# Latent attention's scores: two heads per unit of the order of weights in place of one, its second group one unit later

## The reference, cut to what matters

```python
q_lat = jnp.einsum('bshd,hld->bshl', qh, w_uk)
...
_, idx = lax.top_k(score, k_sel)
...
logits = jnp.einsum('bqhl,bqkl->bqhk', qlb, c_sel).astype(jnp.float32) * (DSA_HEAD_DIM ** -0.5)
...
p = jax.nn.softmax(logits, axis=-1).astype(c.dtype)
o_lat = jnp.einsum('bqhk,bqkl->bqhl', p, c_sel)
o = jnp.einsum('bqhl,hld->bqhd', o_lat, w_uv)
```

## Time and profile before

| what | us |
|---|---|
| median of 3 runs (1111.29 to 1111.47) | 1111.39 |
| span of the profiled execution | 1109.4 |
| TensorE busy in it | 1100.7 (99%) |
| VectorE busy | 744.2 (67%) |
| ScalarE busy | 506.9 (46%) |
| GpSimd busy | 19.8 (2%) |

### The profile page before, as it was taken

The page is one execution under the profiler, slowest core; times in us unless marked ns, Lnnn a source line. Parts: engine busy times, 40 slices in busy tenths (PEclk is TensorE's granted clock), DMA queues, the critical chain, the costliest instruction groups (busy, mean ns, idle before and its releaser), DMA issues.

```text
span 1109.4 us, 18066 instructions
## 1 busy us (share of the span) xinstructions
PE 1100.7 (99%) x7344; PEld 931.1 (84%) x7344; DVE 744.2 (67%) x1195; ACT 506.9 (46%) x851; POOL 19.8 (2%) x40
## 2 busy tenths in 40 slices
PE   9999999999999999999999999999999999999997
PEld 8888888888888888878888887887789999999986
DVE  6875876864686247448789896447568677667853
ACT  7562354324675225533342434336544444444543
POOL 1000000000001001000000000000000000000000
PEclk9999999999999999999999999999999999999999
DMA  9543324432215433522223232231121322333241
GB/s 372 220 149 125 125 68 133 127 102 73 74 58 167 139 95 111 185 74 79 77 76 95 77 95 68 66 114 58 58 73 61 114 93 80 115 115 114 81 186 76
DMA packets 33618, 121.09 MB, mean 109 GB/s; under 512 B 3824, under 2 KB 3824, under 8 KB 33536
## 3 DMA queue, kind: packets, MB, share of 16 engines
q1 hardware_dynamic: 30672, 109.88, 29.7%
q0 software_dynamic: 2720, 10.03, 2.7%
q10 hardware_dynamic: 144, 0.03, 0.0%
HBM read 115.74 MB, written 4.19 MB: 108 GB/s over the span
## 4 chain that ended last, share of the span: by engine, by line
PE 98%; DMA 1%; DVE 1%; ACT 0%; SPq 0%; issue 0%; ACTq 0%
PE acc L1829 22%; PE acc L1831 21%; PE acc L1830 21%; PE acc L1841 2%; PE side L1841 2%; PE acc L1839 2%; PE side L1839 2%; PE acc L1837 2%; PE side L1837 2%; PE acc L2189 2%; PE side L1829 2%; PE side L1830 2%; PE side L1831 2%; PE side L2071 2%; PE side L1984 2%; PE side L2189 1%
## 5 line engine op out<-in xcount | busy, mean ns | idle before, releaser
L1160 DVE TENSOR_TENSOR w_lo<-raw,w_hi 128x1024 fp32r<-128x1024 f32 (+2 forms) x194 | 225.8, 1165 | 149.7 <-ACT w_hi L649 146.8
L1829 PE MATMUL acc<-hT_hi,w_hi 128*128 128x512 f32 x648 | 258.9, 400 | 0.0
L1831 PE MATMUL acc<-hT_hi,w_lo 128*128 128x512 f32 x648 | 252.8, 390 | 0.0
L1830 PE MATMUL acc<-hT_lo,w_hi 128*128 128x512 f32 x648 | 252.4, 390 | 0.0
L649 ACT ACTIVATE w_hi<-raw 128x1024 fp32r<-128x1024 f32 (+2 forms) x194 | 195.6, 1009 | 115.4 <-PE acc L1831 87.7
L1829 PEld LDWEIGHTS acc<-hT_hi,w_hi 128*128 128x128 f32 x648 | 121.9, 188 | 26.9 <-issue 2.9
L1831 PEld LDWEIGHTS acc<-hT_hi,w_lo 128*128 128x128 f32 x648 | 121.6, 188 | 26.1
L1830 PEld LDWEIGHTS acc<-hT_lo,w_hi 128*128 128x128 f32 x648 | 121.9, 188 | 23.6
L1829 PE MATMUL acc<-w_hi,hT_hi 128*128 128x512 f32 (+1 forms) x152 | 60.3, 396 | 0.0
L1831 PE MATMUL acc<-w_hi,hT_lo 128*128 128x512 f32 (+1 forms) x152 | 58.8, 387 | 0.0
L1830 PE MATMUL acc<-w_lo,hT_hi 128*128 128x512 f32 (+1 forms) x152 | 58.7, 386 | 0.0
(11 more groups left out here) (461 smaller groups left out, 2251.5 us busy)
## 6 DMA issues: line engine op xcount, KB each, us to landing
raw<-in_ga SPq DMA_DIRECT2D x32, 512.0 KB, 4.5
ada_raw<-in_ada SPq DMA_DIRECT2D x16, 512.0 KB, 11.5
raw<-in_wo SPq DMA_DIRECT2D x16, 512.0 KB, 3.5
raw<-in_br SPq DMA_DIRECT2D x16, 512.0 KB, 3.5
raw<-in_q SPq DMA_DIRECT2D x8, 512.0 KB, 3.5
raw<-in_u SPq DMA_DIRECT2D x8, 512.0 KB, 4.0
raw<-in_gp SPq DMA_DIRECT2D x8, 512.0 KB, 4.5
raw<-in_ada_w SPq DMA_DIRECT2D x8, 512.0 KB, 3.6
```

The source lines that it names most:

```text
L1160: nc.vector.tensor_tensor(out=lo[:, 0:width], in0=strip_of(k), in1=hi[:, 0:width].bitcast(f32), op=ALU.subtract).then_inc(lo_made, 1)
L1829: nc.tensor.matmul(ps, w[0], x[0], start=first, stop=False)
L1830: nc.tensor.matmul(ps, w[0], x[1], start=False, stop=False)
L1831: return nc.tensor.matmul(ps, w[1], x[0], start=False, stop=last)
```

## The change

```diff
-    SCORES_AT[(1, 9, 19, 27)[_s // 4] + _s % 4 if _s < SPARSE else 38 + (_s - SPARSE) // 2].append(_s)
+    SCORES_AT[(1, 10, 19, 27)[_s // 4] + _s % 4 // 2 if _s < SPARSE else 38 + (_s - SPARSE) // 2].append(_s)
```

## The result

The changed kernel takes 1123.74 us (median of 4 executions, 1123.54 to 1124.94) against 1111.39 before (median of 4 executions, 1111.29 to 1111.47): 12.35 us more, a ratio of 1.0113 with a 95% interval of 1.0102 to 1.0125. Forecast were 1119.8 and a range up to 1123.0. The sign was right, and the time lies above the range.

The account below looks back on a forecast made before the run. PE, busy 99% of the span, was taken as the bound. Stops 0.4 + 3.5 + 2.4 + 0.5 + 2.6 + 0, less gains 0.45 and 0.5, make 8.45 us: 1111.39 + 8.4 = 1119.8, range 1116.0 to 1123.0.

Parts of the forecast that it names:

- The stops: In slots with two turns, PE's second turn waits until ACT has copied the first out of bank side2.
- slot 2: Between turn 0 and turn 1, ACT's round trip of 0.73 us leaves PE a stop of 0.4 us.
- slot 3: Turn 3 waits for ACT's copy, which stands behind DVE's layer norm statistics: stop 3.5 us, between 3.1 and 3.9.
- slot 11: Turn 5 waits for ACT's copy, which stands behind DVE's gate product: stop 2.4 us, between 1.5 and 2.8.
- slot 12: Turn 7 waits for ACT's copy, by the same computation as slot 11: stop 0.5 us.
- slot 20: Turn 9 waits for ACT's copy, made later by slot 19's second score: stop 2.6 us, between 2.0 and 3.0.
- Slot 21: No stop, as ACT has no result to take out and PE three things ahead, 1.65 us.
- The 0.45 at `sel`: In slot 27, PE's wait for the top-k result goes: 0.3 us shown idle and 0.16 more, 0.45 won.
- fewer switches: Eight of sixteen logits no longer have a panel behind them, 0.09 us each: 0.5 us won, between 0 and 0.7.
- The clock falls: Rival: slot 3's 3.5 us stop lowers TensorE's clock; 1122.5 us with half a panel slowed, 1125 whole; chance 0.06.
- catch up: Rival: PE's stops give DVE and ACT time; slot 3's stays, others halve or nearly go: 1116 to 1117.4 us; chance 0.10.
- only the round trip counts: Rival: prompt ACT copies leave stops of 0.2 to 0.5 us; if PE hides these too, 1110.4 us; chance 0.05.

Follow-up runs that it names:

- a wait alone: Kernel before, no score moved, with PE waiting at the end of slot 3's side work until ACT has copied that slot's turn: 1116.47 us.
- two halves: Changed kernel, with the two turns of a slot in blocks 0 and 1 put into the two halves of bank side2: 1115.3 us.
- three-block kernel: Kernel before, with blocks 0, 1 and 3 paired, block 3 from slot 28, and blocks 0 and 1 using both halves of side2: 1111.12 us.
- filled kernel: Changed kernel, with matmuls of no use in the stops, 13 in slot 3 and 9 in slot 20: 1120.69 us.
- kernel with the copies first: Changed kernel, with ACT copying the turns before its wait for DVE's statistics in slot 3 and gate product in slots 11, 12, 20: 1112.98 us.
- block 0 alone: Kernel before, with only block 0's scores two to a slot (slots 1, 1, 2, 2): 1116.94 us.
- half-filled: Changed kernel, with 5 matmuls of no use in slot 3's stop and 9 in slot 20's: 1122.46 us.
- copies of slot 3 first: Changed kernel, with ACT making slot 3's copies of the turns before it waits for DVE's statistics: 1119.45 us.
- block 2 alone: Kernel before, with only block 2's scores two to a slot (slots 19, 19, 20, 20): 1115.2 us.

## Why the prediction was right or wrong

**The stops.** Right, in place, cause and size. Forecast and measured, in us: slot 2, 0.4 and 0.40; slot 3, 3.5 and 3.49; slot 11, 2.4 and 2.36; slot 12, 0.5 and 0.50; slot 20, 2.6 and 2.68; slot 28, 0 and no wait in the list. In slot 3 both ends of the stop came 0.25 us later than forecast, so its length stayed. Slot 21 was given nothing, because ACT has no result to take out and PE three things ahead, and lost 0.26: the forecast left out that the copy waits for the first of PE's two sums there to free the buffer. The cause of the five stops is shown: a wait alone costs the same, two halves of the bank take it away, and so does the order of ACT's queue.

**What is won.** The 0.45 at `sel` was right. The 0.5 for fewer switches was not there. In the changed kernel the logits that follow logits in slot 1 take 0.28 us to their last product (497.90 to 498.18) where the first take 0.22: part of the switch is paid at the next float32 product, be it a panel's or a score's. In the three-block kernel, with six of the eight switches gone, 0.16 us is left, no more than its noise.

**The sum.** Without the clock the changed kernel stands 9.2 us over the one before (filled kernel), where the sum said 8.45. That would have been 1120.6, inside the range. Two ends of terms do not follow from what the prediction says, though nothing rests on them: slot 11's own bounds for the second score (0.4 and 1.5) give a stop of 2.2 to 3.3, not 1.5 to 2.8, and the low ends of all terms add up to 5.85 at the least, not 5.7.

**The clock.** This is the step that failed. "The clock falls" was a rival with 6 in 100 and had to be part of the forecast: it costs 3.05 us at the median and 4.5 in the profiled execution, and the sum had nothing for it. Two things in that step were wrong. From 2 us of idle at 1.00 at the end of the program it took that an idle of 2 us "leaves" the clock; the row only says that the clock had not fallen yet within those 2 us, and the runs show that it falls after PE has resumed, behind an idle shown as 2.16 us. It looked at slot 3 alone, though slot 20's stop was forecast at 2.6. Its price for one fall, half a panel slowed or 2.7 us, was fair, where the slowed stretches cost 1.3 to 2.8 each; the whole panel, 5.5, was too much. The Trainium skill, TensorE: Matmul & The Clock Gate, "HAM oscillation", has it that the work behind a wait of PE starts at the lower clock. The trace agrees behind slot 3's stop, 0.50 at 514.55; behind slot 20's the work starts at 1.00 and the fall comes within 0.8 us of it, and behind the added wait of 3.19 us shown there is none in the profiled execution. So the page names the right danger, but it does not follow every stop, and the measurements decide.

**The rivals.** DVE and ACT did not catch up: slot 11 was 2.36 us late, even with DVE rid of score 4 in slot 9. The kernel with the copies first comes near "only the round trip counts", and shows what the change would have cost with a prompt ACT: 1.2 us over before, not a gain, as the second turn still waits in slots 2, 3 and 12 (and 21), for the causes given above.

**What would have shown it.** The waits are in the list as foreseen (slot 21's is too short for it), the one for `sel` is gone, and no `w_lo` is waited for. "The granted clock is 1.00 in slots 3 and 4" is the line that the trace contradicts.

## What to carry to other kernels

Before two uses of one bank are put into the same slot, find the copy that frees it in the timeline of the engine that makes it, and read when it starts, not how long it takes: here a copy of 0.26 us came 3.6 us late, because it stood behind a wait for a third engine, and cost nothing only as long as a whole panel lay between. Look also for the second condition of that copy, here that a sum has read the buffer it writes. On a kernel that TensorE bounds, stops as long as these (2.3 to 3.5 us) are to be priced with the clock behind them: 1.3 to 2.8 us more where it fell, which differed from stop to stop and from execution to execution. Matmuls put into the stop took that part back. And an idle shown in the timeline of pipelined matmuls is short by the overlap, here 0.16 us each.

## What the runs showed of the hardware that was not expected

- Behind idles of PE shown as 2.2 to 3.3 us the granted clock fell to 0.50 at some and not at others. In the profiled executions it fell behind slot 3's stop (changed kernel, block 0 alone, half-filled), slot 11's (half-filled) and slot 20's (changed, two halves, copies of slot 3 first). It stayed at 1.00 behind slot 11's stop (changed, filled, copies of slot 3 first), slot 20's (block 2 alone) and the added wait of 3.19 us. By their times, executions of one kernel differ in it too: block 2 alone in two groups 1.5 us apart.
- Behind the idles shown as 2.2 to 2.5 us, where it fell, it fell only after PE had resumed its work (five cases); in the two idles of 3.33 us it fell before.
- Matmuls of no use made the changed kernel 3.05 us faster and brought the spread of its executions from 1.4 to 0.2 us.
